# Router logits from rows not yet divided by their norm: transposes and logits placed inside the output products, root and shift applied to the logits

## The reference, cut to what matters

```python
x = x + gate * (o @ w_out)
h = rms_norm(x, norm_ffn) * (1 + scale) + shift      # adaLN: scale, shift from the condition c
scores = jax.nn.sigmoid(h @ router_w)                # 16 logits for each row
sel = scores + router_bias                           # best group, then its two best experts
for e in range(N_EXPERTS):
    he = jax.nn.silu(t @ w_gate[e]) * (t @ w_up[e])
    y = y + combine[:, e:e + 1] * (he @ w_down[e])
```

## Time and profile before

| | us |
|---|---|
| median of 3 runs | 1464.72 (1463.73 to 1470.1) |
| span of the profiled execution | 1464.9 |
| PE busy | 1280.1 (87%) |
| DVE busy | 1101.5 (75%) |
| ACT busy | 693.7 (47%) |
| layer 0: `project_out` on PE from 448.79, router's first row on DVE at | 519.91 |
| layer 1: `project_out` on PE from 1050.32, router's first row on DVE at | 1121.44 |

### The profile page before, as it was taken

The page is one execution under the profiler, slowest core; times in us unless marked ns, Lnnn a source line. Parts: engine busy times, 40 slices in busy tenths (PEclk is TensorE's granted clock), DMA queues, the critical chain, the costliest instruction groups (busy, mean ns, idle before and its releaser), DMA issues. The chain is left out here.

```text
span 1464.9 us, 15502 instructions
## 1 busy us (share of the span) xinstructions
PE 1280.1 (87%) x6000; PEld 970.2 (66%) x6000; DVE 1101.5 (75%) x1324; ACT 693.7 (47%) x890; POOL 311.9 (21%) x129
## 2 busy tenths in 40 slices
PE   4798997859899959999999967986898799999992
PEld 1476885659884557888888754444446588888882
DVE  2757986667783657999999946967357499999994
ACT  2222344222251316777777714227522377777770
POOL 2100000000000001555555310000000145555541
PEclk9799998979999959999999977997996799999997
DMA  9788626011703257999999546354006499999955
GB/s 328 259 266 272 214 96 211 19 44 58 259 2 130 87 219 273 375 391 382 373 378 373 225 157 240 115 203 183 1 29 258 142 358 385 377 381 392 380 206 191
DMA packets 63856, 338.17 MB, mean 231 GB/s; under 512 B 11837, under 2 KB 12350, under 8 KB 49700
## 3 DMA queue, kind: packets, MB, share of 16 engines
q1 hardware_dynamic: 51428, 311.00, 57.3%
q0 software_dynamic: 11536, 22.91, 4.5%
q10 hardware_dynamic: 816, 3.23, 0.6%
HBM read 325.64 MB, written 28.84 MB: 242 GB/s over the span
## 5 line engine op out<-in xcount | busy, mean ns | idle before, releaser
L1421 PE MATMUL ps<-ring_r,work_r 128*128 128x512 f32 x536 | 212.7, 397 | 0.0
L2455 DVE TENSOR_TENSOR ring_r<-ring,early_mod_r 128x2048 fp32r<-128x2048 f32 x76 | 188.7, 2512 | 21.2 <-ACT early_mod_r L1576 20.7
L1419 PE MATMUL ps<-early_mod_r,work_r 128*128 128x512 f32 x468 | 187.8, 401 | 7.7 <-DVE work_r L2758 4.7
L834 POOL TENSOR_TENSOR work<-work,early_mod 128x1024 f32<-128x1024 f32 x30 | 158.1, 5271 | 157.3 <-ACT work L1576 157.3
L1576 ACT ACTIVATE work<-ps 128x512 f32<-128x512 f32 (+3 forms) x121 | 80.5, 670 | 224.8 <-PE ps L1421 134.7
L1420 PE MATMUL ps<-early_mod_r,work_r 128*128 128x512 f32 x468 | 183.1, 391 | 0.0
L1576 ACT ACTIVATE work_r<-ring 128x2048 fp32r<-128x2048 f32 (+2 forms) x87 | 133.8, 1558 | 89.2 <-PE ps L946 89.2
L1576 ACT ACTIVATE early_mod_r<-ring 128x2048 fp32r<-128x2048 f32 x79 | 147.6, 1910 | 0.3 <-PE ps L1421 0.3
L937 PE MATMUL ps<-const,work 128*128 128x128 f32 x712 | 106.4, 293 | 44.2 <-DMA work<-h_rows,row_i 11.9
L1419 PE MATMUL ps<-work_r 128*128 128x512 f32 x324 | 132.9, 410 | 6.8 <-DVE work_r L2758 4.7
L937 PEld LDWEIGHTS ps<-const,work 128*128 128x128 f32 x712 | 90.1, 151 | 68.7 <-issue 15.0
(11 more groups left out here) (330 smaller groups left out, 2448.3 us busy)
## 6 DMA issues: line engine op xcount, KB each, us to landing
ring<-in_moe_w_up_dram SPq DMA_DIRECT2D x33, 2048.0 KB, 10.8
early_mod<-in_ada_w_dram SPq DMA_DIRECT2D x80, 512.0 KB, 4.4
ring<-in_moe_w_gate_dram SPq DMA_DIRECT2D x19, 2048.0 KB, 9.6
hT<-in_moe_w_down_dram SPq DMA_DIRECT2D x16, 2048.0 KB, 9.9
ring<-in_moe_w_down_dram SPq DMA_DIRECT2D x15, 2048.0 KB, 10.2
work<-in_moe_w_gate_dram SPq DMA_DIRECT2D x14, 2048.0 KB, 10.8
ring<-in_ab_w_in_dram SPq DMA_DIRECT2D x7, 2048.0 KB, 10.4
ring<-in_ada_w_dram SPq DMA_DIRECT2D x4, 2048.0 KB, 23.6
```

The source lines that it names most:

```text
L834: return nc.gpsimd.tensor_tensor(yb[buf], yb[buf], mod[:, 5 * D:6 * D], ALU.mult)
L1419: mm(out, a_lo, w_hi, start=first_, stop=False)
L1421: return mm(out, a_hi, w_lo, start=False, stop=last_)
L2455: v.tensor_tensor(half_of(l, m, half, True), half_of(l, m, half), highs[(2 * m + half) % MHIGHS].bitcast(F32), ALU.subtract).then_inc(SV.s ...
```

## The change

The rows are no longer normed before they are transposed. DVE multiplies each half of a tile's `x` with `s` as soon as that half is there (`u_rows`, a product of 128x512). PE transposes it by halves of four (`turn_half`), each in the middle of the eight matmuls of a later output product. ACT moves six of a tile's eight transposed blocks and DVE two (`put_half`) to `uT`, which has two buffers. The logits of tile t - 1 stand on PE between the two products of tile t (`tile_logits`). The shift's logits are computed the same way: `turn_shift` in the first product, eight more matmuls after the second. DVE puts root and shift onto the 16 logits of each row (`tile_logits` on DVE), and `h` itself (`tile_rows`, one operation in place of two) follows. The squares are summed by halves. For the last tile the second half's transposes and half of its logits still come after the last product, and `tile_rows` comes after its logits. The two `expert_high` of the fourth matrix move on ACT behind the exponential, and the two `expert_low` on DVE to later places in `router`. SP's fifth load waits for the last product, not for the logits. `router_w` is laid out on the host in another order, in as many bytes.

```diff
-        hx_tmp = work[:, TT * D:TT * D + D]
+        u_rows = [work[:, far_slot + D * n:far_slot + D * n + D] for n in range(2)]
+        uT = [work[:, far_slot + D * n:far_slot + D * n + D].rearrange("p (k q) -> p k q", k=KD) for n in (2, 3)]
...
-                        sp.wait_ge(RT_PE.sem, RT_PE.at(l, "logits"))
+                        sp.wait_ge(outp_pe.sem, outp_pe.at(8 * l + 7, "job"))
                     elif m == RING + 1:
+                        sp.wait_ge(TN_PE.sem, TN_PE.at(TT * l + TT - 1, "logits"))
                         sp.wait_ge(TN_DVE.sem, TN_DVE.at(TT * l + TT - 1, "h"))
...
+            def turn_shift():
+                for k in range(KD):
+                    ins = turn(bank(6 + k // 4)[:, cols(k % 4)], mod[:, 3 * D + P * k:3 * D + P * k + P])
+                ins.then_inc(SHIFT_PE.sem, SHIFT_PE.one("turned"))
+
+            def turn_half(l, t, n):
...
+                pe.wait_ge(TN_DVE.sem, TN_DVE.at(u, f"u{n}"))
+                if t:
+                    pe.wait_ge(TN_ACT_EV.sem, TN_ACT_EV.at(u - 1, f"ev{n}"))
+                    if n:
+                        pe.wait_ge(TN_DVE_EV.sem, TN_DVE_EV.at(u - 1, "ev1"))
+                elif n:
+                    pe.wait_ge(SHIFT_ACT.sem, SHIFT_ACT.at(l, "ev"))
+                for k in range(4):
+                    dst = bank(6 + k // 2)[:, cols(k % 2)] if n else bank(4)[:, cols(k)]
+                    ins = turn(dst, u_rows[t % 2][:, 512 * n + P * k:512 * n + P * k + P])
+                ins.then_inc(TN_PE.sem, TN_PE.one(f"t{n}"))
+
+            def logits(b, of, half):
+                for k in range(4 * half, 4 * half + 4):
+                    ins = mm(bank(b)[:, 0:NE], of[:, k], router_w[:, k], start=(k == 0), stop=(k == 7))
+                return ins
+
+            def tile_logits(l, t):
+                u = TT * l + t
+                pe.wait_ge(TN_ACT_EV.sem, TN_ACT_EV.at(u, "ev0"))
+                if t:
+                    pe.wait_ge(LOGIT_DVE.sem, LOGIT_DVE.at(l, f"z{t - 2}" if t > 1 else "shift"))
+                logits(LOGIT_BANKS[t % 2], uT[t % 2], 0)
+                if t == TT - 1:
+                    turn_half(l, t, 1)
+                pe.wait_ge(TN_ACT_EV.sem, TN_ACT_EV.at(u, "ev1"))
+                pe.wait_ge(TN_DVE_EV.sem, TN_DVE_EV.at(u, "ev1"))
+                logits(LOGIT_BANKS[t % 2], uT[t % 2], 1).then_inc(TN_PE.sem, TN_PE.one("logits"))
...
+                            if k == 3:
+                                if n:
+                                    turn_half(l, t, 0)
+                                elif t:
+                                    turn_half(l, t - 1, 1)
+                                else:
+                                    turn_shift()
                         ins.then_inc(outp_pe.sem, outp_pe.one("job"))
-                    if t:
-                        turn_tile(l, t - 1)
+                        if n == 0 and t:
+                            tile_logits(l, t - 1)
+                        elif t == 0 and n:
+                            pe.wait_ge(SHIFT_ACT.sem, SHIFT_ACT.at(l, "ev"))
+                            for half in range(2):
+                                ins = logits(LOGIT_BANKS[1], uT[1], half)
+                            ins.then_inc(SHIFT_PE.sem, SHIFT_PE.one("logits"))
                 pe.wait_ge(outp_pe.sem, outp_pe.at(j, "job"))
                 pe.sem_inc(chunk_used, 2)
-                for t in range(TT - 1):
-                    logits(l, t)
-                turn_tile(l, TT - 1)
-                logits(l, TT - 1).then_inc(RT_PE.sem, RT_PE.one("logits"))
+                tile_logits(l, TT - 1)
...
+                def put_half(t, n):
+                    u = TT * l + t
...
+                        act.wait_ge(SHIFT_PE.sem, SHIFT_PE.at(l, "logits"))
+                    src = bank(6, 4, P)[:, 0:2] if n else bank(4, 4, P)
+                    f(uT[t % 2][:, 4 * n:4 * n + (2 if n else 4)], src).then_inc(TN_ACT_EV.sem, TN_ACT_EV.one(f"ev{n}"))
                 table(ACT.Abs_reciprocal_sqrt)
+                act.wait_ge(SHIFT_PE.sem, SHIFT_PE.at(l, "turned"))
+                f(uT[1], ps[:, 6:8].rearrange("p b (k n) -> p (b k) n", k=4)).then_inc(SHIFT_ACT.sem, SHIFT_ACT.one("ev"))
+                    for n in range(2):
+                        act.wait_ge(outp_dve.sem, outp_dve.at(2 * u + n, "x"))
+                        f(junk_wide[:, 512 * n:512 * n + 512], x[:, t, 512 * n:512 * n + 512], ACT.Square, accum_out=half_ss[:, t, n:n + 1]
+                          ).then_inc(TN_ACT.sem, TN_ACT.one(f"ss{n}"))
+                        if n == 0:
+                            put_half(t, 0)
                     act.wait_ge(TN_DVE.sem, TN_DVE.at(u, "var"))
                     f(rstd[:, t:t + 1], var[:, t:t + 1], ACT.Abs_reciprocal_sqrt).then_inc(TN_ACT.sem, TN_ACT.one("root"))
+                    put_half(t, 1)
                     if 0 < t < TT - 1:
-                        put_away(t - 1)
-                for half in range(2):
-                    expert_high(l, 1, half)
-                put_away(TT - 1)
+                        expert_high(l, 0, t - 1)
...
-                act.wait_ge(RT_PE.sem, RT_PE.at(l, "logits"))
-                f(r_e, bank(LOGIT_BANK, TT, NE), ACT.Exp, scale=-1.0).then_inc(RT_ACT.sem, RT_ACT.one("exp"))
+                act.wait_ge(LOGIT_DVE.sem, LOGIT_DVE.at(l, f"z{TT - 1}"))
+                f(r_e, r_e, ACT.Exp, scale=-1.0).then_inc(RT_ACT.sem, RT_ACT.one("exp"))
                 table(ACT.Silu)
+                for half in range(2):
+                    expert_high(l, 1, half)
                 x_high(0)
...
+            def tile_root(l, t):
+                u, c = TT * l + t, slice(t, t + 1)
+                dve.wait_ge(TN_ACT.sem, TN_ACT.at(u, "ss1"))
+                v.tensor_tensor(var[:, c], half_ss[:, t, 0:1], half_ss[:, t, 1:2], ALU.add).then_inc(TN_DVE.sem, TN_DVE.one("sum"))
+                dve.wait_ge(TN_DVE.sem, TN_DVE.at(u, "sum"))
+                v.tensor_scalar(var[:, c], var[:, c], 1.0 / D, EPS, ALU.mult, ALU.add).then_inc(TN_DVE.sem, TN_DVE.one("var"))
                 dve.wait_ge(TN_DVE.sem, TN_DVE.at(u, "var"))
+                if t == TT - 1:
+                    put_half(l, t)
...
+            def tile_rows(l, t):
+                v.scalar_tensor_tensor(out=by_turn(h[:, t], KD), in0=u_rows[t % 2].rearrange("p (q k) -> p q k", k=KD), scalar=rstd[:, t:t + 1],
+                                       in1=mod[:, 3 * D:4 * D].rearrange("p (q k) -> p q k", k=KD), op0=ALU.mult, op1=ALU.add
+                                       ).then_inc(TN_DVE.sem, TN_DVE.one("h"))
+
+            def put_half(l, t):
+                u = TT * l + t
+                dve.wait_ge(TN_PE.sem, TN_PE.at(u, "t1"))
+                v.tensor_copy(uT[t % 2][:, 6:8], bank(7, 4, P)[:, 0:2]).then_inc(TN_DVE_EV.sem, TN_DVE_EV.one("ev1"))
+
+            def tile_logits(l, t):
+                dve.wait_ge(TN_PE.sem, TN_PE.at(TT * l + t, "logits"))
+                v.scalar_tensor_tensor(out=r_e[:, t], in0=bank(LOGIT_BANKS[t % 2])[:, 0:NE], scalar=rstd[:, t:t + 1], in1=shift_logits,
+                                       op0=ALU.mult, op1=ALU.add).then_inc(LOGIT_DVE.sem, LOGIT_DVE.one(f"z{t}"))
...
+                        if t >= 2:
+                            dve.wait_ge(TN_PE.sem, TN_PE.at(TT * l + t - 2, "t1"))
+                        half_ = slice(512 * n, 512 * n + 512)
+                        v.tensor_tensor(u_rows[t % 2][:, half_], xs, s_[:, half_], ALU.mult).then_inc(TN_DVE.sem, TN_DVE.one(f"u{n}"))
+                        if n == 0 and t == 1:
+                            dve.wait_ge(SHIFT_PE.sem, SHIFT_PE.at(l, "logits"))
+                            v.tensor_copy(shift_logits, bank(LOGIT_BANKS[1])[:, 0:NE]).then_inc(LOGIT_DVE.sem, LOGIT_DVE.one("shift"))
+                            dve.wait_ge(LOGIT_DVE.sem, LOGIT_DVE.at(l, "shift"))
+                        if n == 0 and t:
+                            tile_logits(l, t - 1)
+                    tile_root(l, t)
+                    if t < TT - 1:
+                        tile_rows(l, t)
+                        put_half(l, t)
+                        if t:
+                            expert_low(l, 0, t - 1)
+                tile_logits(l, TT - 1)
+                tile_rows(l, TT - 1)
...
-                expert_low(l, 1, 0)
...
-                expert_low(l, 1, 1)
+                expert_low(l, 1, 0)
...
                 v.tensor_copy(ovl_i[:, 8:9], nov).then_inc(R.sem, R.one("ovl"))
+                expert_low(l, 1, 1)
                 dve.wait_ge(R.sem, R.at(l, "ovl"))
```

More of the change, by code:

```diff
@@ L198, in build_block @@
         ss = carve("par", TT)
+        half_ss = carve("par", TT, 2)
+        shift_logits = carve("par", NE)
         var = carve("par", TT)
@@ L246, in build_block @@
         norm_dve = Steps(sem("norm_dve"), ["var", "n1", "n2", "n3", "rstd"] + [f"hx{t}" for t in range(TT)] + ["h0", "h2", "ev0", "ev1", "ev2", "ev3"])
-        TN_ACT = Steps(sem("tile_norm_act"), ["ss", "root"])
```

(36 more changed lines are left out.)

41 lines of the change are left out of this document (8 added, 33 removed).

## The result

| | before | after |
|---|---|---|
| median, runs on the same chip | 1466.99 us (1463.73 to 1470.1, 4 runs) | 1483.97 us (1482.69 to 1485.07, 4 runs) |
| ratio | | 1.0118 [1.0094, 1.0142] |
| span of the profiled execution | 1464.9 | 1481.7 |

What follows compares the result with a forecast made beforehand. PE's dense output products were taken to bound the stage, with DVE setting the pace behind the last. Per layer 9.68 - 7.25 = +2.4 us, +4.9 for both: 1464.7 + 4.9 = 1469.6 us, range 1463 to 1477.

Steps and rivals of the forecast that it cites:

- the last of the working: Profile after: past the router start, everything 2.4 us later to the end of the experts, 4.9 from layer 1 on.
- Edits that I cost at nothing: Moved `expert_low`, `expert_high`, the store of `h` and smaller DVE work, all hidden under other work: 0 us.
- The dense stream: PE's output products: added transposes and four logit blocks of 1.87 us cost their full length, +9.68 us a layer.
- The tail: From DVE's start on the last product to the router: 14.06 us shrinks to 6.8, 7.25 off a layer.
- Rival 1: Logits hide between PE's products, weight loads beside matmuls: -5.05 us a layer, 1454.6 us; chance 0.08.
- Rival 2: Turns and logits behind the last product run at half the clock: +1.3 us a layer, 1472.3 us; chance 0.13.
- Rivals 3 to 5: Clock falls in stream (+6.9 us, chance 0.06); first gather meets expert loads (3 a layer, 0.13); PE waits there (+6, 0.04).

Runs made afterwards that it cites:

- the kernel with its arrays in place: Changed kernel with its 24 new numbers in free router scratch, NPAR 1112 instead of 1136, every array where it was before: 1475.48 us, ratio 1.0065.
- The first two experiments: Changed kernel with NPAR 1144 instead of 1136: 1481.92 us, ratio 1.0072; kernel before with NPAR 1136 instead of 1112: 1479.38 us, ratio 1.0059.
- the first experiment: Changed kernel with NPAR 1144 instead of 1136, so that `work` starts on a multiple of 64 bytes again: 1481.92 us, ratio 1.0072.

## Why the prediction was wrong

**The step that failed** is the last of the working: "then everything 2.4 us later to the end of the experts, and 4.9 from layer 1 on". It holds only if the experts keep their pace, and the "Edits that I cost at nothing" do not even name the one that changed it, `NPAR` from 1112 to 1136, which stands in the diff's first lines. It costs 0.59% (about 8.7 us) alone, and took the time out of the range: without it the kernel would stand at about 1475.3.

The other steps, by the forecast's own terms:

- **The dense stream**, forecast +9.68: 451.22 to 517.55 against 448.79 to 505.85, 66.33 - 57.06 = +9.27 us, the same in layer 1. A block takes 1.70 from its start to that of the next product (466.37 to 468.07), not 1.87; with 1.70 the sum would give 9.0, and the rest stands in the products behind a block, which take 3.52 instead of 3.43 (468.07 to 471.59, 462.94 to 466.37). Weight loads (PEld timeline, after) show why:

```profile
465.94 0.19 PEld L1283 LDWEIGHTS ps<-par,work 128*128 128x128 f32 x1 [0.24 <-issue]
466.37 1.75 PEld L1283 LDWEIGHTS ps<-par,work 128*128 128x128 f32 x15 [0.24 <-issue]
```

  One load of 16 lies under the product ahead, 15 follow each other, as said behind the earlier trace rows. The sum had charged the first too, and it had divided 5.62 us by three, which run to the end of the last pass, with the clock already at 0.50 there; from pass to pass it was 0.112 us before and is 0.112 after. Rival 1 is excluded. The rule of the Trainium skill that loads are pulled ahead of running matmuls (TensorE: Matmul & The Clock Gate, Step-by-step: what each phase is for) agrees for that one load, and no further.
- **The tail**, forecast 14.06 to 6.8: 7.02 in layer 0 (517.55 to 524.57) and 7.58 in layer 1 (1125.85 to 1133.43). The copy of two blocks took the 0.42 chosen, `tile_rows` its 1.95. That the stage's 5.0 us for both layers come so near to the 4.9 forecast is in part luck: the stream gave 0.4 less in each layer, the tail 0.2 and 0.8 more.
- **Rival 2, half the clock in the tail**, given 0.13 and +1.3 a layer: part of it came. In layer 1 the last eight passes cost 0.55 more in the kernel after, and 1.14 with the transposes in the kernel with its arrays in place. In the five profiles of the changed kernel and its variants seven of the ten tails paid, 0.55 to 1.14 us, so the chance was too low. The reason against it, that these stand too soon behind the product, was wrong: the transposes that ran slow at 1121.33 stand 2.2 us behind DVE's start on the last product (1119.14).
- **A clock term nobody had.** Windows of the kernel after, layer 0: stream, tail, router's head, first expert's start and the rest of it, against the earlier trace rows:

```profile
502.20:517.50 15.30, 15.30 (x54) 7.89 (x52) 8.73 (x15) 4.43 (x8) 0.53 (x1) 1.00 0.09 35
517.50:522.20 4.70, 2.74 (x21) 2.35 (x20) 3.35 (x10) 2.50 (x5) 0.00 (x0) 0.99 0.81 265
522.20:529.00 6.80, 0.00 (x0) 0.00 (x0) 6.00 (x21) 5.74 (x7) 0.53 (x1) 0.50 1.01 408
...
546.00:556.00 10.00, 7.07 (x20) 5.60 (x21) 1.23 (x1) 1.02 (x1) 1.43 (x2) 0.50 0.31 91
556.00:566.00 10.00, 9.65 (x45) 7.63 (x44) 3.40 (x2) 2.71 (x3) 0.00 (x0) 0.99 0.63 219
```

  The first expert starts at half the clock in both kernels. Before, seven matmuls ran so (545.92 to 549.08), after, twelve (550.90 to 556.19): five more at 0.43 instead of 0.23 us, 1.0 us. PE started 4.98 us later, the clock rose some 7 us later. It is no price of the change: in layer 1 the kernel before pays more, twelve slow matmuls (1148.03 to 1153.29) against nine after (1159.88 to 1163.85), and 34.61 us from the router to the 25th matmul against 33.92. In layer 0 three of the five profiles of the changed kernel and its variants show 34.4 us or more, two 33.4 and 33.5, as some of the kernel before with arrays moved do.
- **Rivals 3 to 5** did not come: clock 1.00 in the stream (451.2 to 517.5 and 1059.5 to 1125.8), no wait on PE there, and the first gather as before (POOL's and PE's rows, after):

```profile
542.36 1.07 POOL L833 DMA_INDIRECT work<-h_rows,row_i  x1 [17.20 <-DVE work L2793]
...
546.56 1.97 PE L944 MATMUL ps<-const,work 128*128 128x128 f32 x8 [5.90 <-DMA work<-h_rows,row_i]
```

  PE waits 5.90 us for it, against 5.79. The four loads and the gather just miss each other, as forecast: the last load, issued at 524.40, lands 17.6 us later, at 542.0. The halves of the experts' weights that moved stay hidden too.

The sum as it should have been: 2 x (9.27 - 7.04) = 4.5 for the stage, 1.2 for the clock as these two profiles have it (0.55 in the tail of layer 1, 1.36 - 0.69 at the first experts), 8.7 for the place: 14.4 of the 17 measured, within the interval (13.8 to 20.8). The 2.43 us by which the stage starts later in the profile after I leave open: kernels whose instructions and arrays ahead of it are those of before start it between 448.0 and 451.4. The first two experiments, which move all of `work`, start it at 453.57 and 453.95, so a part of the price of the place may lie ahead of the stage; one profile of each does not settle it.

**Left open.** Why the place counts. That it is the operand's place within 512 bytes, relative to the other arrays, fits every run here: in the kernel before `xT`, `heT` and `sg` stand whole multiples of 512 bytes from the slab's start, moves by 64 and 96 bytes (and by 128 in the changed kernel) change the pace, moves by 512 do not. Whether a shorter period would do (256 was not run) and with which access the loads collide no run tells. The loads themselves take as long in either place: 188 ns each before, 188 to 189 with `xT` moved. The Trainium skill (TensorE: Matmul & The Clock Gate, Step-by-step: what each phase is for) says that loading the next weights takes no read bandwidth from the running matmul; the matmul's pitch nevertheless follows the place of the array that is loaded, by up to 2.8%. Why the move of `sg` makes DVE faster and POOL slower is open too. And the loss of the first experiment, 0.72%, is less than the 0.65% and its slower pace (0.5% of some 600 us, 0.2% of the whole) add up to; the interval holds both.

## What to carry to other kernels

A diff also changes the memory map: ask of every new number which arrays it pushes on, and try the old kernel with that push alone. Count the records per busy microsecond in a stretch that the change does not touch; where PE is never idle and the clock is full in both, a different count is a different pace, and no chain of waits will show it. Work that lies under somebody's wait is free; moved into a dense stream it costs its whole length, and what follows an idle stretch must be priced at both clocks.

## What the runs showed of the hardware

Matmuls of 128x512 in fp32r at full clock, with PE never idle, took 0.2267 to 0.2380 us from start to start (means of the classes above), by the place of three arrays in `work`. 96 bytes under the array that is loaded cost 0.006 us of each matmul that loads it and at most 0.0014 of the others; 512 bytes cost nothing. Over the whole kernel the ratio runs from 0.9953 to 1.0088 for the same instructions, wider than the 0.65% that the change itself cost.

A block of 16 passes with 16 moving columns took 1.70 us at the full clock between dense products: 0.112 us from pass to pass, with one weight load of the 16 hidden under the product ahead.
